# Norms that spread a column by a repeated stationary operand, gate rows for both directions at once beside the first head, a reordered start, and signals that ride on their instruction

## The reference, cut to what matters

```python
def rms_norm(x, g):                      # first block, before each mixer and each MLP
    return x * rsqrt(mean(x * x, -1) + 1e-6) * g
def _layernorm(x, g, b):                 # second block, after each mixer and each MLP
    mu = mean(x, -1); var = mean((x - mu) ** 2, -1)
    return (x - mu) * rsqrt(var + 1e-5) * g + b

# first block, per layer: mod_* = silu(c) @ ada_w + ada_b, cut in six
hx = rms_norm(x, norm1_g) * (1 + mod_x[1]) + mod_x[0]     # and hc for the context
x = x + mod_x[2] * mixer(hc, hx)                          # layer 0 hybrid, layer 1 attention
x = x + mod_x[5] * sqrelu_mlp(rms_norm(x, norm2_g) * (1 + mod_x[4]) + mod_x[3], w1, w2)
# second block, per layer
x = _layernorm(ALPHA * x + merged @ w_out, ln1_g, ln1_b)
x = _layernorm(ALPHA * x + square(relu(x @ w1)) @ w2, ln2_g, ln2_b)

# hybrid mixer, layer 0: 4 mLSTM heads, forward and backward; the gates are 16 columns of h @ w_in
g = (h @ w_in)[gates] + gate_b           # input gate and forget gate, for each direction
b = cumsum(log_sigmoid(forget)); a = input - b; m = running max of a, along the direction
# the backward direction runs over the reversed tokens, the context first in both
```

## Time and profile before

| what | value |
|---|---|
| median of three runs | 4370.76 us |
| profiled execution, its span | 4369.62 us, 4367.6 us |
| busy: PE, PEld, DVE | 91%, 76%, 48% |
| busy: ACT, POOL | 34%, 38% |
| mean granted TensorE clock | 0.946 of 2.4 GHz |

### The profile page before, as it was taken

How to read it: one execution, slowest core, us unless ns; L and a number is a source line. 1 busy time by engine, 2 the same in 40 slices (tenths; PEclk the granted TensorE clock), 3 DMA queues, 4 the chain that set the end, 5 groups by cost and what they waited for, 6 DMA issues and landing times.

```text
span 4367.6 us, 62752 instructions
## 1 busy us (share of the span) xinstructions
PE 3994.5 (91%) x20662; PEld 3338.0 (76%) x20662; DVE 2113.3 (48%) x3396; ACT 1506.1 (34%) x2435; POOL 1649.2 (38%) x2044
## 2 busy tenths in 40 slices
PE   4988898999978979999999999899988999998997
PEld 3887887999967766888676778688856767886885
DVE  5566655223347765225737622532357475225235
ACT  3122222111225553222645633322245455333223
POOL 0111123333321105566243345466532433544564
PEclk6999998999989989999999999899989999998998
DMA  4333211111110002222121122122211211322322
GB/s 145 121 131 133 95 49 44 63 63 62 58 45 24 25 13 87 97 93 95 49 73 54 49 87 92 63 97 96 96 60 35 78 54 54 99 90 68 96 92 86
DMA packets 92778, 328.59 MB, mean 75 GB/s; under 512 B 10240, under 2 KB 12544, under 8 KB 92544
## 3 DMA queue, kind: packets, MB, share of 16 engines
q1 hardware_dynamic: 90928, 323.61, 22.3%
q10 hardware_dynamic: 1616, 1.90, 0.1%
HBM read 323.38 MB, written 2.10 MB: 75 GB/s over the span
## 4 chain that ended last, share of the span: by engine, by line
issue 66%; POOL 34%; POOLq 1%
POOL Wl L264 34%; POOLq L259 0%; POOLq L261 0%; POOLq L264 0%; POOLq L147 0%; POOLq L258 0%; POOLq L3306 0%
## 5 line engine op out<-in xcount | busy, mean ns | idle before, releaser
L264 POOL TENSOR_TENSOR Wl<-raw,Wh 128x256 fp32r<-128x256 f32 x2040 | 1649.0, 839 | 2717.9 <-ACT Wh L372 2717.7
L372 ACT ACTIVATE Wh<-raw 128x1024 fp32r<-128x1024 f32 x510 | 540.0, 1059 | 1785.6 <-PE psum L1105 1763.6
L1103 PE MATMUL psum<-Hh,Wh 128*128 128x512 f32 (+1 forms) x2704 | 1048.2, 388 | 83.7 <-DVEq L1955 60.2
L1104 PE MATMUL psum<-Hl,Wh 128*128 128x512 f32 (+1 forms) x2704 | 1023.1, 378 | 0.0
L1105 PE MATMUL psum<-Hh,Wl 128*128 128x512 f32 (+1 forms) x2704 | 1022.4, 378 | 0.0
L1103 PE MATMUL psum<-Gh,Wh 128*128 128x512 f32 (+3 forms) x2032 | 754.9, 371 | 23.7 <-DVEq L1955 15.5
L1105 PE MATMUL psum<-Gh,Wl 128*128 128x512 f32 (+3 forms) x2032 | 746.5, 367 | 0.0
L1104 PE MATMUL psum<-Gl,Wh 128*128 128x512 f32 (+3 forms) x2032 | 746.4, 367 | 0.0
L1103 PEld LDWEIGHTS psum<-Hh,Wh 128*128 128x128 f32 x2704 | 522.5, 193 | 218.8 <-DVEq L1955 67.1
L1105 PEld LDWEIGHTS psum<-Hh,Wl 128*128 128x128 f32 x2704 | 522.7, 193 | 72.6
L1104 PEld LDWEIGHTS psum<-Hl,Wh 128*128 128x128 f32 x2704 | 524.1, 194 | 66.0 <-issue 1.6
(11 more groups left out here) (339 smaller groups left out, 4714.4 us busy)
## 6 DMA issues: line engine op xcount, KB each, us to landing
raw<-in_wstream SPq DMA_DIRECT2D x510, 512.0 KB, 3.3
stage<-in_ada SPq DMA_DIRECT2D x80, 512.0 KB, 4.3
M<-in_ada SPq DMA_DIRECT2D x16, 512.0 KB, 5.3
X<-in_xT SPq DMA_DIRECT2D x1, 2048.0 KB, 12.2
out<-X SPq DMA_DIRECT2D x8, 256.0 KB, 2.0
X<-in_ctxT SPq DMA_DIRECT2D x1, 1024.0 KB, 7.2
M<-in_memT ACTq DMA_DIRECT2D x1, 1024.0 KB, 6.6
M<-in_axial ACTq DMA_DIRECT2D x1, 512.0 KB, 3.5
```

Of the source, the lines that this page charges most:

```text
L264: last = pool.tensor_tensor(Wl[:, s, c], raw[:, s, c], Wh[:, s, c].bitcast(F32), ALU.subtract)
L372: act.activation(Wh[:, s], raw[:, s], ACT.Copy).then_inc(v["w_high"], 1)
L1103: pe.matmul(dst, a[0], b[0], start=first, stop=False)
L1104: pe.matmul(dst, a[0], b[1], start=False, stop=False)
```

## The change

It has five parts.

1. **Spreads without diagonals.** The column itself, repeated 128 times by a stride of zero, is the stationary operand, and the identity is what moves: one 128x128 product for each 128 tokens in place of one product of up to 512 columns. DVE's diagonals (L2000, L2054) go, and M keeps their room. DVE signals PE right after the column is there. In a layer norm the shift is signalled before the variance is worked out.
2. **First stages.** SP loads vec and const under a semaphore of their own, then four ada blocks, then X, then the other ada blocks. PE and the sigmoid wait for the constants alone. DVE adds the squares between the ada rounds 1 to 4, two slices in each.
3. **Gate rows.** Both directions are worked on at once, direction 0 on partitions 0 to 3, direction 1 on 32 to 35 with its row written reversed, so that one forward scan does both. The work is cut in four pieces: `gates_begun` before head 0, `gates_summed` and `gates_ended` within its query and key tiles, `gates_turned` between its value tiles. PE starts head 0 right after the gate projection, turns the rows after the first value tile, and waits for the exponentials only before head 0's products.
4. **Signals.** In `rms`, `centred_sums`, `layer_norm` and `add_gated`, where the next instruction doesn't read the result, the signal rides on the instruction (`then_inc`) and the wait for its own end goes.
5. **MLP.** In `hidden`, DVE signals PE before it gives back the hand buffer.

```diff
 # SP
+            sp.dma_start(vec[:], a["vec"]).then_inc(consts_loaded, 16)
+            sp.dma_start(const[:], a["const"]).then_inc(consts_loaded, 16)
             for n in range(ADA_FIRST):
+                if n == 4:
+                    for dst, src in ((X[:, :, 0:CTX], ...), (X[:, :, X0:TOK], ...)):
+                        sp.dma_start(dst, src).then_inc(loaded, 16)
 # PE
+        def spread_tokens(bank, col):
+            n = col.shape[1]
+            for i in range(n):
+                mm = pe.matmul(psum[:, bank, i * P:(i + 1) * P], col[:, i:i + 1].broadcast_to([P, P]), ident, start=True, stop=True)
+            mm.then_inc(v["spread_done"], 1)
-            for lo, hi, c in SPANS[2 - len(segs):]:
-                wait_ready()
-                pe.matmul(psum[:, 5 - c, 0:hi - lo], ones, diags[:, lo:hi], start=True, stop=True).then_inc(v["spread_done"], 1)
+            wait_ready()
+            for lo, hi, c in SPANS[2 - len(segs):]:
+                spread_tokens(5 - c, v["sc"][:, 40 + lo // P:40 + hi // P])
-        for d in range(2):                      # turned rows, ahead of head 0
-            wait_ready()
-            ...
-        pe.wait_ge(v["rows_done"], 2)
+                if h == 0 and 0 in token_tiles: # behind head 0's first value tile
+                    wait_ready()
+                    b = tiles.take(pe)
+                    for d, row in enumerate(gate_inputs(v)):
+                        for tt in range(6):
+                            ...
 # DVE, rms
             do(dve.reciprocal(roots, take(n)))
+            for_pe()
             give_back()
-            for lo, hi, c in parts:
-                dve.tensor_tensor(diags[:, lo:hi]..., ident..., col..., ALU.mult).then_inc(v["for_pe"], 1)
-                        stt(T[k % 3][:, lo:hi], ...)
-                    for_act()
+                        last = dve.scalar_tensor_tensor(out=T[k % 3][:, lo:hi], ...)
+                    last.then_inc(v["for_act"], 1)
 # DVE, layer_norm
             stt(shift, psum[:, b, 0:4], 1.0 / D, centre, ALU.mult, ALU.subtract)
+            for_pe()
             ...
-            spread_columns(shift_diag, shift)
             do(dve.reciprocal(root, take(4)))
+            for_pe()
             give_back()
-            spread_columns(root_diag, root)
 # DVE, first stages
+            if q == 1:
+                dve.wait_ge(v["loaded"], 32)
+            for k in ADA_SQUARES[q]:            # ((), (0, 1), (2, 3), (4, 5), (6, 7), (), (), ())
+                add_squares(k, ALL_SEGS)
 # DVE, gates
+        def gates_begun():
+            gb = [look(), look()]
+            gate_preactivations(gb, F, 1)
+            stt(T, F, -1.0, F, ALU.mult, ALU.max)
+            for_act()
+            gate_preactivations(gb, A_row, 0)
+            for b in gb:
+                free(b)
+            do(dve.memset(R, 0.0))
```

More of the change, by code:

```diff
@@ L398, in used, with used_beside_ada @@
             return b
-        def used_beside_ada(n, point):
-            for _ in range(n):
+        def used_beside_ada(n, point, turned=False):
+            for i in range(n):
                 b = tiles.look(act)
-                tiles.skip(ada_tiles(point))
+                tiles.skip(ada_tiles(point) + (turned and i == 0))
                 point += 1
@@ L497, in _ @@
         used(2)
-        for d in range(2):
[L499 to L506, removed]
+        act.wait_ge(for_act, wants.next())
+        act.activation(tab[0:36, 0:TOK], tab[0:36, 0:TOK], ACT.Exp, scale=-1.0).then_inc(a_chain, 1)
+        act.wait_ge(a_chain, own.next())
+        give(tab[0:36, 0:512], ACT.Ln, 512, slice(0, 36), bias=sc[0:36, 62:63])
+        give(tab[0:36, 512:TOK], ACT.Ln, TOK - 512, slice(0, 36), bias=sc[0:36, 62:63])
         point = 0
@@ L525, in _ @@
             point = used_beside_ada(2, point)
-            point = used_beside_ada(2, point)
+            if h == 0:
+                act.wait_ge(for_act, wants.next())
+                for d, sums in enumerate((tab[0:4, 0:TOK], tab[32:36, TOK:2 * TOK])):
+                    act.activation(gate_rows(v, d)[1], sums, ACT.Exp, scale=-1.0).then_inc(v["rows_done"], 1)
+            point = used_beside_ada(2, point, turned=h == 0)
             fill = 0
@@ L1171, in layer_stats @@
             column_sums(b, 4, S1).then_inc(v["tile_done"], 1)
-            _, (_, shift_diag, root_diag), _, _ = layer_norm_scratch(v)
-            spread(6, shift_diag)
-            spread(4, root_diag)
+            _, (_, shift, _, root), _ = layer_norm_scratch(v)
+            spread(6, shift)
+            spread(4, root)
         def rms_stats(segs, at=1024):
@@ L2197, in _ @@
         rms(ALL_SEGS, 0, 0, 0)
[L2198 to L2205, removed]
-            for_act()
+        T, F, A_row = tab[0:36, 0:TOK], tab[0:36, TOK:2 * TOK], arow[0:36, :]
@@ new lines, in gate_preactivations, with scan @@
+        def gate_preactivations(gb, dst, at):
+            for d in range(2):
+                bias = vec[0:4, VEC["gate_b"] + 2 * d + at:VEC["gate_b"] + 2 * d + at + 1]
+                for j, lo, hi, to, step in gate_pieces(d):
+                    ts(dst[32 * d:32 * d + 4, to][:, ::step],
+                       psum[64 * d + 32 * at:64 * d + 32 * at + 4, gb[j], lo - j * HALF:hi - j * HALF], bias, ALU.add)
+        def scan(dst, src, second, op0, op1):
+            init = 0.0
+            for s in segments:
+                do(dve.tensor_tensor_scan(dst[:, s], src[:, s], second[:, s], init, op0, op1))
+                init = dst[:, s.stop - 1:s.stop]
@@ L2294, in _ @@
                     (normed, gated)[j](h - 1)
+                elif j == 0:
+                    gates_summed()
+            if h == 0:
+                gates_ended()
             values(look(), 0, 4, P)
```

170 lines of the change are left out of this document (93 added, 77 removed).

## The result

The changed kernel takes 4307.76 us (median; 4302.72 to 4309.05, 4 runs), the kernel before beside it 4368.83: a ratio of 0.9858 with a 95% interval of 0.9838 to 0.9878. The forecast was 4287 (4268 to 4306), so the direction was right and over a quarter of the gain is missing: 84 were forecast, about 61 came.

A forecast was written before the change was run, and what follows sets the result against it. PE, busy 91%, was taken to lose time unfed, waiting on DVE in norms, DVE and ACT in gates. Terms 10.4 + 30 + 16.1 + 19.2 + 7.2 + 1 = 83.9 off 4369.6 gave 4285.7, median 4287 (4268 to 4306).

The forecast's parts named there:

- First stages: Start of the kernel: PE starts at 6.4 us and ends its ada passes at about 38, not 48.5; gain 10.4 us.
- Gates: Gate projection to head 0's products: gate work fits beside head 0's projections, 36.5 us in place of 66.45; gain 30 us.
- 24 turning passes: Head 0, between the value tiles: 2.7 us, until 28.3 us behind the gate projection; second values and ada then take 7.0.
- Rival (B): Gates or start give back part: DVE 8 to 16 us late in head 0, or slow ada blocks; 4294 to 4303; chance 0.14.
- Spreads: Norms, without diagonals: 1.15 us in three RMS norms, 0.95 in the other; 0.95 and 1.85 in two layer norms each.
- Signals: Riding signals save 3.3 us in three RMS norms, 1.85 in another, 3.4 per layer norm, 1.8 per centred sum; MLPs 1.
- rival (C): First 61.5 us and gates: PE's clock comes up sooner, so more comes off; gain over 97 us, 4270; chance 0.06.

The follow-up runs named there:

- turn_late_vf: Changed kernel with head 0's first values split ahead of the gates' columns and its 24 turning passes behind the second value tile: 4300.67 us, 0.984.
- values_first: Changed kernel with DVE splitting head 0's first tile of values before it works out the gates' columns: 4305.38 us, 0.9846.
- busy: Changed kernel with three more products of 512 columns, into a bank nobody reads, behind the 24 turning passes: 4302.74 us, 0.9845.
- turn_late: Changed kernel with head 0's 24 turning passes behind the second tile of values instead of ahead of it: 4296.62 us, 0.9833.

## Why the prediction was right or wrong

**First stages (10.4 forecast).** 8.7 in the pair of traces, 7.4 to 7.9 by undoing, of which 3 to 5 show in the times. PE's first product came at 7.53 instead of 6.4: the constants, behind vec, landed 4.2 after their issue and not in the 3.2 of the earlier trace rows. DVE's four rounds ended at 34.7 where I had 33.2. The last columns ended at 40.45, forecast 38, before 48.46. The step that was off is the end: behind DVE's last adds a whole round of PE still stood, 32 passes of 2.15 us from 36.50 and the columns from 38.58, and I had allowed the DMA alone as a bound there.

**Gates (30 forecast).** 19.3 came by product 288, and 15 to 18 by undoing them. The step that failed is "24 turning passes (2.7 at this clock)... second values and ada 7.0": I priced all of head 0 at the full clock. The bank of the first values was free 30.8 us behind the gate projection (97.17), 2.1 later than forecast; but then the clock was at half, and from there to the products it took 13.9 us (to 111.08) where I had 7.8. The half clock lasted on to 116.45, and by product 288 the loss was 10.7. The rest of the path was sound: the earlier trace rows gave the tiles, the bank wait of 2.05 at 73.58 was forecast as 2, and with the passes moved the same arithmetic holds to half a microsecond (37.0 against 36.5). The row that should have warned me is the one I used as a price: before, these passes ran at half clock. I took the idle time around them for the cause and carried only the duration over. Rival (B) had the right size (8 to 16 us back), and by its own sign, products over 42 us behind the projection, it came true at 44.7; but it named the wrong engine: DVE was late by 0.89 (at 78.93) and 1.62 us only, and taking the latter away brought nothing.

The other part of the miss, 4 us, stood in no step: one tile fewer shifts the ring of banks at a loop's entry 620 us later. The prediction costed the gate tile's bank where it is held, not the count.

**Spreads (10.0 forecast).** 8 to 13 measured. Twelve passes took 2.93 us and 16 took 3.67: less the 0.3 of latency 0.219 and 0.211 each, forecast 0.215. The weight load between the passes adds nothing, with 140 of them in the kernel. From the shift to the second scaling 3.98 us instead of 5.88: 1.90, forecast 1.85.

**Signals (32.6 forecast, and 1 for the MLPs).** 30 to 36 measured for the first; no run takes the MLPs' signal apart. A k of the layer norm takes 2.04, forecast 2.07; of the RMS norm 2.34, forecast 2.37. The first RMS norm gained 6.7 instead of 4.4; in its trace PE's clock comes up at 55 us, within it, a small part of rival (C). The centred sums gave less than 1.8: the next add starts 0.61 after the subtraction, as forecast, but two of the three shown take longer for it:

```profile
4260.57 0.69 DVE L2051 TENSOR_TENSOR X<-X,psum 128x512 f32<-128x512 f32 x1
4261.18 1.21 DVE L1929 TENSOR_TENSOR S<-S,hand 128x512 f32<-128x512 f32 x1
4262.53 0.69 DVE L2051 TENSOR_TENSOR X<-X,psum 128x512 f32<-128x512 f32 x1
4263.13 1.09 DVE L1929 TENSOR_TENSOR S<-S,hand 128x512 f32<-128x512 f32 x1
4264.37 0.69 DVE L2051 TENSOR_TENSOR X<-X,psum 128x512 f32<-128x512 f32 x1
4264.98 0.68 DVE L1929 TENSOR_TENSOR S<-S,hand 128x512 f32<-128x512 f32 x1
```

POOL splits weights from 4260.23 to 4263.67, so over the first two and not the third; that these 0.4 to 0.5 us come from the split was read from the overlap and not tested. The Trainium skill (SBUF — State Buffer, Who interferes with whom) says that a VectorE instruction with both inputs in SBUF competes with GpSimd's reads, and one with an input in PSUM doesn't; the rows agree, since the subtractions from psum stay at 0.69.

**The sum.** Against the profiled pair 17.0 us are missing of 83.9: gates 15.1 (10.7 in head 0, 4.4 at the ring), first stages 1.7, and about 3 scattered; the norms brought 2.7 more. The norms' 2.7 and the scattered 3 are within what two executions differ by, and stay open one by one: the same code between two places varied by up to 5.5 us from trace to trace (products 864 to 1271 took 103.8 to 109.3 us, with 10.2 to 20.5 us of half clock in them).

**The range.** By the medians 23 us are missing, not 17: the execution that was profiled (4302.72) was the fastest of its four, and it lies inside the range. The range ended 1.8 us short of the median. It had the gates' loss in it (rival B, 0.14), but not together with a shorter first stage and a second loss.

## What to carry to other kernels

Price a stretch of PE work with the clock that it will meet, and ask it of every run of few-column passes, even one without waits: here 24 of them cost 2.8 us themselves and about 8 behind them. A short wait beside small passes can do the same (turn_late_vf). In this kernel the passes were cheaper behind the last projection tile than ahead of it; try such places, and read the clock's row behind them before counting a gain. Where buffers are taken in a ring that loops reset, a tile added or taken away anywhere ahead changes the wait at the next loop's entry; compare PE's longest waits by the count of products in both traces, since these losses lie far from the edit.

## What the runs showed of the hardware

- The granted clock fell to half among 24 four-column passes with no wait of PE ahead of them (values_first, at 95.7 us; they start at 94.56), and, in turn_late_vf, among small ada passes behind a wait of 1.36 us, ahead of the 24. It stayed at half while PE was busy with 128-column passes in 10.53 of 10.53 us (from 97.17 in the changed kernel). It came back with three products of 512 columns (busy, 100.3). In turn_late, 128-column passes that began at the full clock kept it over 5.41 us.
- More work made a stage shorter: with three unused products (4.54 us) product 288 comes 52.8 us behind the gate projection, in place of 58.7 and 60.2. Of the whole kernel's time this shows only as 2 to 3.6 us, across sets.
- A signal that rides on a DVE instruction lets the next one start 0.07 to 0.08 us before its end (0.61 after the start of one of 0.69, 0.67 after one of 0.75).
- A column repeated by a stride of zero as the stationary fp32 operand costs PE no more than a plain one: 0.211 us a pass of 128 columns at half clock, where the plain ones of the earlier trace rows have a pitch of 0.108 at the full clock, twice which is 0.216.
